# A two-block model kernel: constants in two loads, another order of four projections, earlier copies and rounding

## The reference, cut to what matters

```python
def first_block(...):
    h = rmsnorm(x, norm_mix)
    (q, kc, vc, ks, vs, kw, vw, nsa_g, rq, rk, rv, rg, gate_a, gate_b) = split(h @ w_in)
    # rotary on q, kc, ks, kw; compression of keys and values, 15 windows of 32 tokens:
    blk = k[cmp_idx] + pe                         # 15 windows, overlapping by half
    k_cmp = silu(blk @ w1) @ w2                   # and v_cmp the same way
    # three attentions per query head (compressed, selected, window), gated by sigmoid(nsa_g)
    # retention: rotary on rq, rk, then (rq rk^T * decay) rv, normalised per head
    ret_out = silu(rg) * ret
    mix = sigmoid(gate_a) * (nsa_out @ w_proj_a) + sigmoid(gate_b) * (ret_out @ w_proj_b)
    x = x + mix @ w_out
    x = x + square(relu(rmsnorm(x, norm_mlp) @ w_up)) @ w_down
    return rmsnorm(x, norm_final)

def second_block(...):                            # on the first block's output
    z, xBC, dt, q, k, v, r, a1, g_ssd, g_gla = split(rmsnorm(h) @ w_in_2)
    xBC = silu(causal_conv(xBC))                  # 4 taps, 1536 channels
    dt = softplus(dt + dt_bias); a = dt * -exp(A_log)
    y = rmsnorm((ssd(xBC, dt, a) + D * x) * silu(z))        # per group of 512
    o = rmsnorm(gated_linear_attention(q, k, v, a1)) * silu(r)
    h = h + (sigmoid(g_ssd) * (y @ w_up_ssd) + sigmoid(g_gla) * (o @ w_up_gla)) @ w_o
    h = h + cross_attention(rmsnorm(h), rmsnorm(mem))
    h = h + (silu(g) * u) @ w_ffn_out             # g, u = split(rmsnorm(h) @ w_ffn_in)
    return rmsnorm(h, norm_final_2)
```

## Time and profile before

| | us |
|---|---|
| three runs | 990.21, 990.55, 991.37 |
| median | 990.55 |
| the profiled execution's own time | 992.43 |
| its span in the profile | 990.40 |
| TensorE busy in the span | 964.87 |
| VectorE busy | 631.81 |
| ScalarE busy | 507.58 |
| GpSimd busy | 52.33 |

### The profile page before, as it was taken

One profiled execution on the slowest core, in us unless ns is written; L12 is line 12 of the kernel. 1 busy time (PEld: TensorE's weight loads), 2 busy tenths in 40 slices (PEclk: granted clock), 3 DMA queues, 4 the chain that ended last, 5 costly groups with the idle time before them and its releaser, 6 DMA issues.

```text
span 990.4 us, 15893 instructions
## 1 busy us (share of the span) xinstructions
PE 964.9 (97%) x6552; PEld 872.5 (88%) x6552; DVE 631.8 (64%) x822; ACT 507.6 (51%) x746; POOL 52.3 (5%) x88
## 2 busy tenths in 40 slices
PE   7999999999999999999999999999999999999996
PEld 5877889989999888988988899998998899999995
DVE  5667576676655555778867687775654556555544
ACT  5565655555544444556545475544555354444442
POOL 4000000002000000300000002100200020000000
PEclk9999999999999999999999999999999999999999
DMA  8974344554665556455554446564745356565651
GB/s 288 328 249 128 94 126 101 171 192 147 215 194 188 184 179 197 121 187 179 166 156 127 131 140 199 156 197 138 228 155 170 120 158 197 179 197 176 196 183 43
DMA packets 134935, 170.36 MB, mean 172 GB/s; under 512 B 7648, under 2 KB 99088, under 8 KB 134864
## 3 DMA queue, kind: packets, MB, share of 16 engines
q1 hardware_dynamic: 133472, 165.47, 54.3%
q10 hardware_dynamic: 848, 2.58, 0.8%
q0 software_dynamic: 544, 1.31, 0.4%
HBM read 168.28 MB, written 1.05 MB: 171 GB/s over the span
## 4 chain that ended last, share of the span: by engine, by line
PE 83%; DVE 8%; ACT 4%; issue 3%; DMA 1%; POOL 0%; SPq 0%; ACTq 0%; DVEq 0%; POOLq 0%
PE ps L356 13%; PE ps L357 13%; PE ps L358 13%; PE ps L386 6%; PE ps L387 5%; PE ps L388 5%; PE ps L693 5%; PE ps L692 5%; PE ps L694 5%; PE ps L339 4%; PE ps L435 3%; DVE room L1430 3%; DVE parts L1396 2%; ACT parts L950 2%; DVE room L1436 1%
## 5 line engine op out<-in xcount | busy, mean ns | idle before, releaser
L1396 DVE TENSOR_TENSOR parts<-raws,parts 128x1024 fp32r<-128x1024 f32 (+1 forms) x308 | 367.9, 1211 | 238.5 <-ACT parts L950 237.5
L950 ACT ACTIVATE parts<-raws 128x1024 fp32r<-128x1024 f32 (+1 forms) x308 | 315.3, 1043 | 252.0 <-PE ps L358 141.8
L356 PE MATMUL ps<-room_r,parts 128*128 128x256 f32 x1248 | 352.5, 282 | 3.0 <-DVE parts L1396 3.0
L358 PE MATMUL ps<-room_r,parts 128*128 128x256 f32 x1248 | 348.5, 279 | 0.0
L357 PE MATMUL ps<-room_r,parts 128*128 128x256 f32 x1248 | 348.4, 279 | 0.0
L356 PEld LDWEIGHTS ps<-room_r,parts 128*128 128x128 f32 x1248 | 234.6, 188 | 9.0 <-issue 3.9
L357 PEld LDWEIGHTS ps<-room_r,parts 128*128 128x128 f32 x1248 | 234.7, 188 | 1.4
L358 PEld LDWEIGHTS ps<-room_r,parts 128*128 128x128 f32 x1248 | 234.6, 188 | 0.0
L386 PE MATMUL ps<-parts,room_r 128*128 128x512 f32 (+1 forms) x336 | 136.2, 405 | 3.0 <-DVE parts L1396 3.0
L387 PE MATMUL ps<-parts,room_r 128*128 128x512 f32 (+1 forms) x336 | 131.6, 392 | 0.0
L388 PE MATMUL ps<-parts,room_r 128*128 128x512 f32 (+1 forms) x336 | 131.5, 391 | 0.0
(11 more groups left out here) (191 smaller groups left out, 843.2 us busy)
## 6 DMA issues: line engine op xcount, KB each, us to landing
raws<-in_w_in SPq DMA_DIRECT2D x100, 512.0 KB, 4.2
raws<-in_w_ffn_in SPq DMA_DIRECT2D x44, 512.0 KB, 4.0
raws<-in_w_up SPq DMA_DIRECT2D x32, 512.0 KB, 4.3
raws<-in_w_down SPq DMA_DIRECT2D x32, 512.0 KB, 4.2
raws<-in_w_ffn_out SPq DMA_DIRECT2D x22, 512.0 KB, 4.3
raws<-in_w_xkv SPq DMA_DIRECT2D x16, 512.0 KB, 4.3
raws<-in_w_out SPq DMA_DIRECT2D x8, 512.0 KB, 4.2
raws<-in_w_up_ssd SPq DMA_DIRECT2D x8, 512.0 KB, 5.4
```

The costliest lines, as they stand in the source:

```text
L356: e.matmul(ps, wh, hT[0][:, k, :], start=k == 0, stop=False)
L358: last = e.matmul(ps, wl, hT[0][:, k, :], start=False, stop=k == K - 1)
L950: e.activation(t.h, t.raw, ACT.Copy).then_inc(s["hi"], 1)
L1396: e.tensor_tensor(t.l, t.raw, t.h.bitcast(F32), ALU.subtract).then_inc(s["lo"], 1)
```

## The change

1. `consts` is loaded in two parts. Its table `decay` (1024 of 1806 columns) moves to the end and comes by a second transfer, issued by ACT after the compression copies, with its own semaphore that DVE waits for at its first use.
2. The four projections run as rq, rk, rg, rv and not as rq, rk, rv, rg. ACT's evacuation of rg, which is a Silu, moves with it.
3. ACT copies `("win", 0)` ahead of qT and kT. DVE's rotations of rq and rk move behind both `windows` steps.
4. ACT copies `cT` ahead of tiles and projections that stood before it.
5. In the convolution, two tiles are issued on ACT and DVE ahead of `y` and of `conv(1)`, and one or two ahead of the Silu and the softplus.
6. TensorE's last `y_out` comes one filling piece later, and so do the four `o_T`. The number of pieces between the neighbouring stages stays as it was.
7. POOL issues the five loads of `rows` after the retention's norms.

```diff
-CONSTS = dict(upper=128, after=128, causal=128, cmask=30, crow=2, decay=1024, inv=72, keep=256, strips=30, own=8)
+CONSTS = dict(upper=128, after=128, causal=128, cmask=30, crow=2, inv=72, keep=256, strips=30, own=8, decay=1024)
...
+        early = offsets(CONSTS)[0]["decay"][0]
@@ tensor
-            fill = chain(*(tm(name, w_in, 1304 + 512 * i, 512, xT, x_ready(MIX), True)
-                           for i, name in enumerate(("rq", "rk", "rv", "rg"))),
+            fill = chain(*(tm(name, w_in, c0, 512, xT, x_ready(MIX), True)
+                           for name, c0 in (("rq", 1304), ("rk", 1816), ("rg", 2840), ("rv", 2328))),
...
-            step(2)
+            step(3)
             y_out(1, 1)
-            step(2)
+            step()
             need(s["wa2"], 16)
...
                 ends(last, ("o", j), b)
+                if j == 1:
+                    step()
                 if j:
                     o_T(j - 1)
             o_T(3)
-            step(3)
+            step(2)
@@ scalar
-            e.dma_start(consts[:, :], a["consts"]).then_inc(s["consts"], 16)
+            e.dma_start(consts[:, 0:early], a["consts"][:, 0:early]).then_inc(s["consts"], 16)
...
                 yield from tm_out(rk, "rk", 1, MIX)
+                yield from tm_out(rg, "rg", 1, MIX, ACT.Silu)
                 yield from tm_out(rv, "rv", 1, MIX)
-                yield from tm_out(rg, "rg", 1, MIX, ACT.Silu)
 
             put_behind(projections())
-            for t in range(2):
-                copy_out(qT[:, :, t * P:t * P + P], chunks(psum[:, where["qT", t].bank, :], 4), ("qT", t))
-            copy_out(kT, halves(psum[:, where["kT"].bank, :]), "kT")
             for i in range(2):
                 full(("win", i))
...
+                if i == 0:
+                    for t in range(2):
+                        copy_out(qT[:, :, t * P:t * P + P], chunks(psum[:, where["qT", t].bank, :], 4), ("qT", t))
+                    copy_out(kT, halves(psum[:, where["kT"].bank, :]), "kT")
+            e.dma_start(consts[:, early:], a["consts"][:, early:]).then_inc(s["decay"], 16)
...
-            copy_out(pcT[0:120, :], psum[0:120, where["cT"].bank, 0:256], "cT")
+            until(where["cT"].at - 5)
+            e.wait_ge(s["pe"], where["cT"].at)
+            emptied(e.activation(pcT[0:120, :], psum[0:120, where["cT"].bank, 0:256], ACT.Copy), "cT")
...
             conv_in(1)
-            until(where["cv", 2].at + 2)
+            until(where["a1dt"].at + 1)
             for t in range(2):
                 e.wait_ge(s["zrstd"], t + 1)
                 e.activation(x[:, t, :], z[:, t, :], ACT.Copy, scale=rstd[sq_of[MIX2]][t]).then_inc(s["y"], 1)
...
             conv_in(3)
+            until(where["cv", 3].at + 3)
             silu(0)
@@ vector
-                for name, dst in (("rq", rq), ("rk", rk)):
+                for name, dst, behind_ in (("rq", rq, ("hid", 1)), ("rk", rk, ("hidT", 1))):
                     for t in range(2):
-                        yield where[name, 0, t].at + 4
+                        yield where[behind_].at
...
+                        e.wait_ge(s["decay"], 16)
                         step(tt(RS[:, h, 0:256], bank_of(("RS", h))[:, 0:256], decay[:, h, :], ALU.mult))
...
             conv_in(2)
-            until(where["cv", 2].at + 2)
+            until(where["a1dt"].at + 1)
             conv(1)
...
             conv(3)
+            until(where["cv", 3].at + 3)
             e.wait_ge(s["soft_exp"], 1)
@@ gpsimd
-            for name in ROWS:
-                v = a[name] if name.startswith("norm_final") else a[name][0]
-                e.dma_start(row(name), v.partition_broadcast(P)).then_inc(s["rows"], 16)
...
                 rsqrt_mean(rrs[:, 4 * t:4 * t + 4], rss[:, 4 * t:4 * t + 4], P, "ret_rstd")
+            for name in ROWS:
+                v = a[name] if name.startswith("norm_final") else a[name][0]
+                e.dma_start(row(name), v.partition_broadcast(P)).then_inc(s["rows"], 16)
```

More of the change, by code:

```diff
@@ L36 @@
 SEMS = (
-    "x0", "x1", "ident", "consts", "cols", "rows", "pos", "w1k", "w1v", "w2k", "w2v", "wa2", "mem", "out",
+    "x0", "x1", "ident", "consts", "decay", "cols", "rows", "pos", "w1k", "w1v", "w2k", "w2v", "wa2", "mem", "out",
     "pe", "hi", "lo",
```

## The result

| | before | changed |
|---|---|---|
| executions | 10 | 10 |
| median, us | 991.85 | 987.69 |
| lowest to highest, us | 990.21 to 993.69 | 985.39 to 990.26 |
| profiled execution's own time, us | 992.43 | 986.90 |
| its span, us | 990.40 | 985.00 |

The ratio is 0.9961, with an interval of 0.9950 to 0.9971: the changed kernel is 2.9 to 5.0 us faster. The forecast was a gain of 4.35 us; the medians differ by 4.16. The forecast median of 986.2 started from 990.55, the median of three runs of the kernel before; over ten it is 991.85, 1.3 higher, and the changed kernel's 987.69 is 1.5 above 986.2.

The account below looks back on a forecast made before the run. TensorE, busy 97% of the span, was taken as the bound. Gains of 1.7 (start to attention), 1.4 (convolution), 0.25 (y_out) and 1.0 (o_T) sum to 4.35 us: median 986.2 from 990.55, range 983.3 to 990.0.

Parts of the forecast that it names:

- Start and windows: Kernel start and first windows: earlier weight tiles gain 0.6 us, the new copy and rotation order 1.66, together 2.26.
- cT and rg: First attention steps: 4.85 us of waits and low clock go, about 5.4 comes, a loss of 0.6.
- The two new waits: TensorE waits about 2.5 us for rg's bank ahead of the rq transposes and 2.7 ahead of `probs_T` 0.
- The first rival: Clock falls behind the second new wait, not the first: 1.6 us more lost, gain 2.75, median 987.8; chance 0.17.
- The prediction's 1.6: Cost in us of the low clock around the four score matmuls and eight transposes at the cT wait before.
- The slow side: TensorE stays at the low clock from `probs_T` 0 to scores 3: 8.3 us more, median 994.5; chance 0.05.
- Convolution: Waits worth 3.24 us go, 1.85 comes back: gain 1.4, bounds 0 (DVE-bound, chance 0.16) and 3.2 (0.09).
- The third stall I listed: In the convolution, a returning TensorE stall of 0.35 us at the bank of an SSD copy.
- y_out: In the GLA, one piece later hides a loss of 1.02 us at 555.47; gain 0.25, between 0 and 1.0.
- that matmul is no earlier: In the GLA, the matmul that the scan's four DVE operations await has as many pieces ahead, limiting the gain to 0.25.
- o_T: A filling piece placed before the last wait, ahead of 604.16, gains 1.0 us, between 0.5 and 1.1.
- Drains: Table switches hide a drain beyond their load, some 1.3 us at each new wait: gain 1.75, median 988.8; chance 0.03.

Follow-up runs that it names:

- e6: e2 with ACT's copies of qT and kT ahead of the windows' and DVE's rotations at their old place; median 983.73 us.
- e7: e2 with the constants in one load and the five row loads at their old place; median 984.61 us.
- e9: e2 with both the loads and the windows' order as before the change; median 986.37 us.
- e4: The changed kernel with the last y_out at its old place, one filling piece earlier; median 987.62 us.
- e12: e2 without its early Exp activation, so only Silu's table load is in idle time; median 986.86 us.
- e3: The changed kernel with the convolution's four orders as before the change; median 989.28 us.
- e10: e2 with the convolution's four orders as before the change; median 986.95 us.
- e11: e2 with the copy of cT again behind tile 27, rg's evacuations and tiles 28 and 29; median 984.83 us.
- e1: The changed kernel with projections and evacuations again in the order rq, rk, rv, rg; cT still copied first; median 985.96 us.
- e2: The changed kernel plus two unread one-column activations, Silu and Exp, that pull both table loads into ACT's idle time; median 984.25 us.
- e5: e2 with the last y_out and the four o_T at their places of before the change; median 985.91 us.
- e8: e2 with ACT and DVE reordered further around rg's evacuations, tiles 27 to 29, the maxima and first exponentials; median 982.10 us.

## Why the prediction was right, and where its steps were not

- **Start and windows (2.26 forecast, 2.14 in the profile).** Right in sum, wrong in the parts. I gave 0.6 to the loads and 1.66 to the order. ACT's timeline of before, and then of the changed kernel, has the last tile of 1024 columns ahead of the Sin chain (its idle time ended by the transfer):

```profile
26.60 1.06 ACT L950 ACTIVATE parts<-raws 128x1024 fp32r<-128x1024 f32 x1 [4.54 <-DMA raws<-in_w_in]
```

```profile
24.06 1.06 ACT L953 ACTIVATE parts<-raws 128x1024 fp32r<-128x1024 f32 x1 [2.18 <-DMA raws<-in_w_in]
```

It came 2.54 us earlier, and by itself this removes the windows' wait, as the order by itself does (e6, e7, e9). In the eleven profiles with the loads as in the changed kernel the same row stands between 23.80 and 24.71, in e7 and e9, with the loads as before, at 25.35 and 26.44. The step that failed is that I followed the earlier tile only to its first wait at 35.67 and not on through DVE's rotation to the next one.
- **cT and rg (scores 3 ahead by 1.7 forecast, 1.46 in the profile).** The two new waits came where they were placed and `probs_T` 0 at 101.13 (101.0 forecast). The first is 2.24, not 2.5. The second is 1.10 and not 2.7, because the clock fell in between and the wait absorbed it, as the prediction said for that case; in e4's profile, with the clock up between them, it is 2.66.
- **The clock.** The first rival, a fall behind the second wait, is not one case against the forecast but happens in some executions: e4's profile, whose kernel is the same up to the GLA, has it. Its price there was 2.9, and 1.5 in e12. The prediction's 1.6 is 1.5 by its own rows (half of 1.97, and 1.23 less 0.70). The changed kernel's times from 985.39 to 990.26 fit such a mixture, though the timeline of only one of its executions was kept: the mean granted clock over the span is 0.993 in the two slowest (989.68 and 990.26), as in e4's profile, and 0.995 to 0.998 in the other eight. It does not explain all, since the next slowest (989.11) has 0.996. Of the ten waits of 1.88 to 2.66 us that the fourteen profiles have behind the windows, eight were followed by a fall: 1.97 in before, 2.24 in the changed kernel, 2.24 and 2.33 in e3, 2.66 in e4, 2.32 in e10, 1.88 in e11 and 2.65 in e12. Two were not: 2.32 in before and 2.24 in e4. No wait of up to 1.63 was (e1, e2, e5 to e9).
- **The slow side** (clock low all the way to scores 3) is in no profile. The longest low stretch is e4's, some 6.8 us.
- **Convolution (1.4 forecast, 2.02 measured).** The mis-sized term is the time that comes back: I had 1.85 us, and it was the waits of 0.25 and 0.69 with their ends, 1.2. The third stall I listed did not come.
- **y_out (0.25 forecast, 0.57 by e4 and e5).** The step that failed is "that matmul is no earlier". The number of pieces ahead of it was the same, but the wait for `y_out` had stood ahead of it too. The matmuls that the four DVE operations wait for, in e2 and then in e5:

```profile
554.43 1.99 PE L340 MATMUL ps<-room,wa 16*128 16x256 f32 x8
```

```profile
555.17 1.99 PE L340 MATMUL ps<-room,wa 16*128 16x256 f32 x8
```

Counted from the first transposes behind the convolution (465.95 and 465.90), they begin 0.79 earlier in e2.
- **o_T (1.0 forecast, 1.13 measured).** Right.
- **Drains.** None, as the row of before at 108.07 had it.

The profile's sum is larger than the forecast (5.6 against 4.35) and the median is not (4.16). The difference of two profiles holds the chances of two executions. That the median's gain is within 0.2 of the forecast is in part luck: two terms were too small by 0.6 and 0.3, and executions in which the clock stays low longer pull the other way. This remains open: how much of the median's gain in the changed kernel is due to falls it adds at 92 or 101 and how much to the one it saves at 438.

## What to carry to other kernels

Before crediting an edit with a wait, follow every other edit of the change that starts earlier down to the same wait; two of them can remove it twice, and then undoing one shows nothing. Where an activation of another table sits on the path, a one-column activation of the same function in the idle time ahead of it moves the load there. And kernels whose waits are all short were mostly steadier: those without a wait above 1.7 us (e1, e2, e5 to e9) spread over 0.5 to 1.9, those with a wait of 1.88 or more over 2.9 to 4.9, except e10, whose five executions lie within 0.23 in spite of its 2.32. So test single parts on such a base.

## What the runs showed of the hardware that was not expected

The start of the projections differs between executions. In e12 two successive matmuls behind the start, and the stretch around them:

```profile
13.18 0.63 PE L388 MATMUL ps<-parts,room_r 128*128 128x512 f32 x1
...
13.61 0.63 PE L389 MATMUL ps<-parts,room_r 128*128 128x512 f32 x1
```

```profile
13.00:14.00 1.00, 1.00 (x3) 0.75 (x3) 1.00 (x2) 0.76 (x4) 0.00 (x0) 1.00 0.94 358
```

The same stretch in e2, where the matmuls are as far apart:

```profile
13.00:14.00 1.00, 1.00 (x4) 0.71 (x4) 1.00 (x2) 0.76 (x4) 0.00 (x0) 0.50 0.99 377
```

The matmuls are 0.43 us apart, twice the usual 0.23. That is the step of the low level: the changed kernel has it from 93.01 to 95.57, at a granted clock of 0.50. So the 1.00 in e12's row is not the clock that TensorE had. In the nine profiles whose matmuls are slow from the first one on, this stretch reads 1.00; in the five that start at 0.23 and then turn slow (e2, e4, e6, e9, e10), it reads 0.50. At the start of a profile the distance of the matmuls has to be read, and not the clock's column alone.

There are six such steps in before, after and e8, twelve in e1 and e11, thirteen in e12 and five to eight in the rest. At 0.19 to 0.20 each that is up to 1.5 us between executions from the start alone; e1, e11 and e12 are the ones whose lead at 42 us is negative (-0.53, -0.41 and -0.86 against 0.18 to 0.78 in the others).

The second is that the length of a wait does not decide alone: a single wait of 1.88 us (e11) was followed by a fall, one of 2.32 (before) was not. The fall can begin more than 1 us after the work has resumed: in the changed kernel the transposes start at 91.68, 92 to 93 us still reads 0.94, and 93 to 94 reads 0.50.
